# The head of a two-block transformer kernel: its set-up stages become the beginning of the input projection's stage

## What is computed

```python
def rmsnorm(x, g, eps=NORM_EPS):
    xf = x.astype(jnp.float32)
    y = xf * lax.rsqrt(jnp.mean(xf * xf, axis=-1, keepdims=True) + eps)
    return (y * g.astype(jnp.float32)).astype(x.dtype)

def modulate(h, shift, scale):
    return h * (1.0 + scale) + shift

def adaln(cond, w_mod, b_mod):
    return jax.nn.silu(cond) @ w_mod + b_mod
...
        mod = adaln(c, w_mod[l], b_mod[l])[:, None, :]
        mod_c = adaln(c_ctx[None, :], w_mod[l], b_mod[l])[:, None, :]
...
        h = modulate(rmsnorm(x, p['g_pre_mix']), sh1, sc1)
        h_c = modulate(rmsnorm(ctx, p['g_pre_mix']), sh1c, sc1c)
        y, y_c = token_mixer(h, h_c, p, lam_init, cos, sin, need_ctx)
```

## Time and profile before

| | us |
|---|---|
| median of 3 runs | 3788.89 |
| the runs | 3785.69 to 3792.41 |
| the profiled execution's own time | 3778.42 |
| its span from the first instruction to the last | 3776.4 |

### The profile page before, as it was taken

The page is one execution under the profiler, slowest core; times in us unless marked ns, Lnnn a source line. Parts: engine busy times, 40 slices in busy tenths (PEclk is TensorE's granted clock), DMA queues, the critical chain, the costliest instruction groups (busy, mean ns, idle before and its releaser), DMA issues.

```text
span 3776.4 us, 71939 instructions
## 1 busy us (share of the span) xinstructions
PE 3500.4 (93%) x30972; PEld 3214.3 (85%) x30972; DVE 2033.0 (54%) x3196; ACT 1569.3 (42%) x2561; POOL 122.8 (3%) x233
## 2 busy tenths in 40 slices
PE   5299987999988998999999999999999999999997
PEld 2288776988987877887888999989999999999997
DVE  1447775878774774553434687332224653344665
ACT  0455664444433773443333555211114443333553
POOL 0000000000000000100000011000000100000011
PEclk8599998999998998999999999999999999999998
DMA  4223344232323403321111565211113421111664
GB/s 149 83 79 127 119 149 171 88 105 88 104 74 67 93 1 113 122 79 51 45 51 56 188 210 189 77 28 45 45 45 108 134 84 46 45 45 56 196 218 140
DMA packets 323386, 369.44 MB, mean 98 GB/s; under 512 B 14189, under 2 KB 262716, under 8 KB 323070
## 3 DMA queue, kind: packets, MB, share of 16 engines
q1 hardware_dynamic: 306958, 311.48, 26.8%
q0 software_dynamic: 16112, 53.37, 4.2%
HBM read 303.84 MB, written 60.95 MB: 97 GB/s over the span
## 4 chain that ended last, share of the span: by engine, by line
PE 55%; DVE 3%; ACT 2%; issue 1%; DVEq 0%; DMA 0%; POOL 0%; ACTq 0%
PE psum L3252 10%; PE psum L3253 9%; PE psum L3254 9%; PE psum L2331 4%; PE psum L2806 4%; PE psum L2332 4%; PE psum L2333 4%; PE psum L2807 4%; PE psum L2808 4%; PE psum L2668 1%; DVE u_val L3452 1%; DVE w_lo L3153 1%; PE psum L3199 1%; ACT u_val L3343 0%; DVE g L3457 0%
## 5 line engine op out<-in xcount | busy, mean ns | idle before, releaser
L3252 PE MATMUL psum<-mix_h_hi,w_hi 128*128 128x342 f32 (+5 forms) x1848 | 636.1, 344 | 17.1 <-DVE w_lo L3153 15.2
L3253 PE MATMUL psum<-mix_h_hi,w_lo 128*128 128x342 f32 (+5 forms) x1848 | 632.1, 342 | 0.0
L3254 PE MATMUL psum<-mix_h_lo,w_hi 128*128 128x342 f32 (+5 forms) x1848 | 631.6, 342 | 0.0
L2198 DVE TENSOR_TENSOR w_lo<-w_raw,w_hi 128x1024 fp32r<-128x1024 f32 (+1 forms) x167 | 195.8, 1172 | 398.0 <-ACT w_hi L2188 396.5
L3252 PEld LDWEIGHTS psum<-mix_h_hi,w_hi 128*128 128x128 f32 x1848 | 348.9, 189 | 47.4 <-DVE w_lo L3153 18.6
L2188 ACT ACTIVATE w_hi<-w_raw 128x1024 fp32r<-128x1024 f32 (+1 forms) x167 | 170.3, 1020 | 487.7 <-PE psum L2808 325.3
L3254 PEld LDWEIGHTS psum<-mix_h_lo,w_hi 128*128 128x128 f32 x1848 | 348.8, 189 | 26.9
L3253 PEld LDWEIGHTS psum<-mix_h_hi,w_lo 128*128 128x128 f32 x1848 | 349.0, 189 | 26.2
L737 PE MATMUL psum<-h_hi,w_hi 128*128 128x512 f32 (+1 forms) x592 | 228.3, 386 | 49.2 <-DVE w_lo L899 49.2
L2331 PE MATMUL psum<-down_ghi,w_hi 128*128 128x256 f32 x944 | 269.8, 286 | 0.4 <-DVE down_glo L2203 0.2
L3329 ACT ACTIVATE xs<-psum 128x1024 f32<-128x1024 f32 (+1 forms) x66 | 67.8, 1028 | 486.4 <-PE psum L3254 486.4
(11 more groups left out here) (437 smaller groups left out, 8064.6 us busy)
## 6 DMA issues: line engine op xcount, KB each, us to landing
w_raw<-in_w_down SPq DMA_DIRECT2D x118, 512.0 KB, 3.9
w_raw<-in_w_up SPq DMA_DIRECT2D x110, 512.0 KB, 3.8
w_raw<-in_w_in SPq DMA_DIRECT2D x59, 512.0 KB, 4.0
down_w_raw<-in_w_down SPq DMA_DIRECT2D x58, 512.0 KB, 3.9
unit<-rw_operands SPq DMA_DIRECT2D x40, 512.0 KB, 6.8
rw_operands<-step_set SPq DMA_DIRECT2D x16, 1024.0 KB, 6.4
mod_w<-in_w_mod POOLq DMA_DIRECT2D x32, 512.0 KB, 5.8
w_raw<-in_w_out SPq DMA_DIRECT2D x32, 512.0 KB, 4.0
```

Source lines behind the costliest of these rows:

```text
L3252: nc.tensor.matmul(out, k.w_hi[:, s, w], xh[:, kk, x], start=(kk == 0), stop=False)
L3253: nc.tensor.matmul(out, k.w_lo[:, s, w], xh[:, kk, x], start=False, stop=False)
L3254: last = nc.tensor.matmul(out, k.w_hi[:, s, w], xl[:, kk, x], start=False, stop=(kk == KD - 1))
```

## The change

The six stages are gone. Their work is written into the class `Front`, whose methods are called at the head of each engine's list in `in_projection`, so that no barrier stands between them and the first tile:

- SP asks for token rows first: five 512 KB buffers (RING), then the four parameter vectors that are needed early (72 rows, EARLY), the other five tiles, three groups of `w_mod` (three buffers), the first `w_raw`, the fourth group, and then the store of x and the constants. The other 36 parameter vectors are asked for by POOL.
- PE turns the ten tiles of tokens first, then spreads the factors, then sums the modulation rows.
- ACT no longer copies halves of `xT` (DVE copies whole tiles). It squares the token rows as they land, with a sum along the row (`accum_out`), so the channel tiles are neither squared nor added up, and PE's sums over channels (L362) are gone.
- DVE multiplies x by the spread factors straight from PSUM into `x_hat`, for all eight tiles and before the modulation is known. `rbc` is not written.
- Scale and shift are applied in place on `x_hat`, even tiles by DVE and odd ones by ACT. Tile 0 of the projection takes the channel tiles as the outer loop and its three pieces inside, and waits for each `h_lo` (`lowered`).
- The late parameter rows are turned between the modulation sums and tile 0, and copied to `prm` by DVE after the last `h_lo`. DVE's `weight_low(1)` and its preparations stand behind that.
- The two memsets of `xs` are gone. Tiles 1 to 25 and all later stages are as they were.

The diff, cut to its core:

```diff
+    def sync(self, sp, first_weights):
+        k = self.k
+        for n in range(self.RING):
+            self.load_tile(sp, n)
+        sp.wait_ge(self.ident_set, 1)
+        for name, src, n, at in self.early:
+            sp.dma_start(self.stage[at:at + n, 0, :], src).then_inc(self.early_landed, 16)
+        for n in range(self.RING, self.n):
+            self.load_tile(sp, n)
+        for n in range(3):
+            self.load_mod(sp, n)
+        first_weights(0)
+        self.load_mod(sp, 3)
+        sp.wait_ge(self.kept, self.n)
+        sp.dma_start(*tiles_of(k.x_dram, k.xT[:, :, CTX:ALL])).then_inc(self.x_stored, 16)
...
+    def scalar_early(self, act):
+        nc, k = self.nc, self.k
+        for n in range(self.n):
+            act.wait_ge(self.row_landed[n % self.RING], 16 * (n // self.RING) + 16)
...
+            nc.scalar.activation(self.junk[n % 2][:, :], self.rows[n % self.RING][:, :], ACT.Square,
+                                 accum_out=k.stat[:, 0, n:n + 1]).then_inc(self.squared, 1)
...
+    def scalar_late(self, act):
+        nc, k = self.nc, self.k
+        act.wait_ge(self.mod_kept, 5)
+        for kk in range(KD):
+            if kk % 2:
+                for c0, c1, gain, shift in self.sides(kk):
+                    nc.scalar.activation(self.hat(kk, c0, c1), self.hat(kk, c0, c1), ACT.Identity, bias=shift, scale=gain)
+                act.drain()
+            else:
+                act.wait_ge(self.shifted, kk // 2 + 1)
+            nc.scalar.activation(k.h_hi[:, kk, :], self.hat(kk, 0, ALL), ACT.Copy).then_inc(self.high, 1)
...
+    def vector_late(self, dve):
+        nc, k = self.nc, self.k
+        self.shift(dve, 0)
+        for kk in range(KD):
+            if kk % 2 == 0 and kk + 2 < KD:
+                self.shift(dve, kk + 2)
+            self.lower(dve, kk)
+        dve.wait_ge(self.late_turned, 1)
...
+        dve.drain().then_inc(self.late_kept, 1)
+        dve.wait_ge(self.x_stored, 16)
...
-            for n in range(TOTAL):
+            front.tensor(pe)
+            pe.wait_ge(w_low, 1)
+            for kk in range(KD):
+                pe.wait_ge(front.lowered, kk + 1)
+                w = slice(kk * P, (kk + 1) * P)
+                for j, (c0, cn) in enumerate(pieces(0)):
...
+            pe.wait_ge(front.late_kept, 1)
+            pe.wait_ge(front.tables, 32)
+            for n in range(1, TOTAL):
...
-            weight_low(0)
-            weight_low(1)
...
-    setup_stage(nc, k)
-    adaln_stage(nc, k, "mod1", 0, 16)
-    load_turned(nc, k, "x", [(ins["ctx"][0], CTX, 0), (ins["x"][0], SEQ, CTX)], k.xT)
```

More of the change, by code:

```diff
@@ L148, in rows_of @@
     return k.prm[:, c:c + 1] if isinstance(c, int) else k.prm[:, bass.ds(c, 1)]
[L151 to L204, removed]
@@ L220, in adaln_turn @@
     return last
[L223 to L274, removed]
@@ L277, in load_turned @@
[L277 to L296, removed]
-                pe.wait_ge(landed[n % 2], 16 * (n // 2 + 1))
-                if n >= 2:
-                    for half in kept:
-                        pe.wait_ge(half, n - 1)
-                for kk in range(KD):
-                    last = nc.tensor.transpose(k.psum[:, 2 * (n % 2) + kk // 4, (kk % 4) * P:(kk % 4) * P + m],
-                                               rows[n % 2][0:m, kk * P:(kk + 1) * P], k.ident[0:m, 0:m])
-                last.then_inc(turned, 1)
-        def halves(half):
-            for n, (src, m, at, r) in enumerate(tiles):
-                out = dst[:, 4 * half:4 * half + 4, at + r:at + r + m]
-                src_ps = k.psum[:, 2 * (n % 2) + half, :].rearrange("p (a b) -> p a b", a=4)[:, :, 0:m]
-                yield n, out, src_ps
-        @block.vector
-        def _(dve):
-            for n, out, src_ps in halves(0):
-                dve.wait_ge(turned, n + 1)
-                nc.vector.tensor_copy(out, src_ps).then_inc(kept[0], 1)
-        @block.scalar
-        def _(act):
-            for n, out, src_ps in halves(1):
-                act.wait_ge(turned, n + 1)
-                nc.scalar.activation(out, src_ps, ACT.Copy).then_inc(kept[1], 1)
@@ L592, in stores @@
                     store_centred(p, s - 1)
-            weights(0)
+            front.sync(sp, weights)
             sp.dma_start(k.cos[:, :], k.ins["cos_k"]).then_inc(tables, 16)
@@ L723, in after_piece @@
                         mean(p, s - 2)
-            for n in range(TOTAL):
+            front.tensor(pe)
+            pe.wait_ge(w_low, 1)
+            for kk in range(KD):
+                pe.wait_ge(front.lowered, kk + 1)
+                w = slice(kk * P, (kk + 1) * P)
+                for j, (c0, cn) in enumerate(pieces(0)):
+                    x, out = slice(c0, c0 + cn), k.psum[:, j, 0:cn]
+                    mm(out, k.w_hi[:, 0, w], k.h_hi[:, kk, x], start=(kk == 0), stop=False)
+                    mm(out, k.w_lo[:, 0, w], k.h_hi[:, kk, x], start=False, stop=False)
+                    last = mm(out, k.w_hi[:, 0, w], k.h_lo[:, kk, x], start=False, stop=(kk == KD - 1))
+            last.then_inc(acc_done, 1)
+            pe.wait_ge(front.late_kept, 1)
+            pe.wait_ge(front.tables, 32)
+            for n in range(1, TOTAL):
                 s = n % 2
@@ L1030, in rope_low @@
                     in1=k.qk_hi[:, 0:m].bitcast(F32), op0=ALU.mult, op1=ALU.subtract).then_inc(worked, 1)
+            front.vector_early(dve)
+            weight_low(0)
+            front.vector_late(dve)
+            weight_low(1)
             c = k.col["k_a"]
@@ L1101, in first_block @@
     k.xT = k.at("x_t", [KD, ALL], k.BIG)
[L1103 to L1106 removed]
+    k.h_hi = k.at("h1_hi", [KD, ALL], 104576, F32R)
     k.h_lo = k.at("h1_lo", [KD, ALL], 104576 + KD * ALL * 4, F32R)
     assert k.top <= k.limit, (k.top, k.limit)
[L1109 to L1119 removed]
     in_projection(nc, k)
```

291 lines of the change are left out of this document (177 added, 114 removed).

## The result

| | us |
|---|---|
| the changed kernel, median of 4 runs | 3677.48 (3673.22 to 3683.83) |
| the kernel before beside it, median of 4 runs | 3790.65 (3785.69 to 3794.36) |
| ratio | 0.9704, 95% interval 0.9684 to 0.9723 |
| the changed kernel's profiled execution, its span | 3679.61, 3677.6 |
| the profiled execution before, its span | 3778.42, 3776.4 |

The kernel is 113 us faster by these medians and 99 by the two profiled executions. The forecast was 97, and its range ended at 3681, 3.5 us too high. Two things have to be found: where the head differs from the forecast, and why two ways of comparing differ by 14 us.

The account below looks back on a forecast made before the run. PE bounds the kernel from tile 1 on, after a head of one-engine stages. Tile 1 moves from 186.3 to 88.4 (24.1 + 3.4 + 3.9 + 32.05 + 25), less 1.0 debt: 3788.9 - 96.9 = 3692, range 3681 to 3707.

Parts of the forecast that it names:

- The turning: Head's start: PE transposes ten token tiles at the low clock, 1.70 us each, from 5.3 us; last copy at 24.1.
- the scatter of the runs: Whole-time range: the runs' own scatter was allowed 3 us at each end.
- The bound and the question: Whole kernel: PE bounds it from tile 1 on, so an earlier tile 1 (186.3 to 88.4) moves everything behind it forward.
- T: Time in the head when the last copy of xT ends, forecast at 24.1 us.
- The rival: Turning in the head: the clock rises among transposes, copies set the pace, T 3 us earlier, total 3689; chance 0.14.
- From T to the modulation: Head: PE idle 3.4 us, spreading matmuls 3.9, modulation sums 32.05; modulation complete at 63.4, no w_mod load in the path.
- From the modulation to tile 1: Head's end: ACT's rounding, scale and shift chain (18.0), then w_lo of tile 1; 25 us, so tile 1 at 88.4.
- The debt: Behind tile 1's start: tile 2's weights come late through single-buffered w_raw, delaying sigmoid and gate product; loss 1 us (0 to 4).
- The low-clock rival for tile 0: Tile 0 of the projection: PE runs it at the low clock, eight channel tiles take 25.6 us, total 3698; chance 0.12.
- POOL's transfers: Late parameter rows: 36 issues at 0.51 us, landed in time; rival of late rows, at 6 us each 3840, chance 0.02.
- the rule of the Trainium skill that the prediction weighed: POOL's 36 transfers: VectorE in a 2-port mode locks GpSimd out of its SBUF rings, which speaks against moving them there.
- The sum and the range: Whole time: 97.9 less 1.0 gives 96.9 us off the median 3788.9, so 3692; range 3681 to 3707.

## Why the prediction was off, point by point

Two terms of the sum failed. The turning was priced with every transpose at the low clock, 1.70 us a tile, and this made it 3.5 us too long. And the scatter of the runs was put at 3 us, where executions of one kernel lie 26 us apart. The points in order:

- **The bound and the question.** Right: the gain is the shift of tile 1, and apart from scatter everything behind it moved as one block. The forecast of that shift was 97.9, measured 103.0. The spans from tile 1 to the end were to be equal within 2 us, and in the two profiles they differ by 4.2 (3590.1 and 3594.2); this too is scatter, of a size that the prediction didn't allow for.
- **The turning (T = 24.1, measured 19.9).** Two terms. The first tile landed 0.7 us sooner than taken. The larger, 3.5 us, was the pace: 1.70 us a tile at the low clock, where the turning took 14.1 us of PE's time from its first transpose to its last, and not 17.6. This is the step that was wrong in its mechanism. The rival had it, with T = 21.2 and a chance of 0.14, and it happened. The rows read for it, 80 transposes at 0.50, showed transposes with gaps of 0.7 to 2.0 us behind the first 16, and I had noted that the change takes the gaps away. The runs with two and five buffers, in either kernel, show that this decides. The rival was off in part in what sets the pace once the clock is up, the copies by its account. They do stand close together, DVE being busy 9.3 of the 10 us from 8 to 18, but from 11.95 on PE waited four times for token rows (1.3 us in all), and the last tile's turning began at 17.56, as its row landed. The working had that landing at 17.7. So with the clock up the transfers, at some 400 GB/s by the windows, set the end of the turning.
- **From T to the modulation (39.35, measured 39.7).** Right in its path, and its sum is right since two errors cancel: PE waited 2.8 us from T to the spreading where 3.4 was taken, the spreading took 4.63 where 3.9 was taken, all of it at 0.50, and the modulation sums 32.3 instead of 32.05. No transfer of w_mod was late; the products x_hat were done at 38.7, before the second group's additions.
- **From the modulation to tile 1 (25, measured 23.7).** The mechanism was right, ACT's chain and then the meeting of PE's end and `w_lo` of tile 1, 0.35 us apart. ACT's pair of scale and shift took 1.72 (rows 6 gave 1.83 as a sum of two durations, and they overlap by a little at their ends), four times, and the whole of ACT's chain 16.9 where 18.0 was taken. The small sums of this part run 0.1 to 0.2 over their terms; nothing hangs on that.
- **The debt (1 us, measured as PE's wait of 0.6).** Right in kind. The low-clock rival for tile 0 did not happen: the clock was back at 1.00 before its third channel tile.
- **POOL's transfers.** Issued at 0.51 to 0.54 each beside a busy DVE (the first took 0.66, the last 0.58), and PE didn't wait for the late rows. The row of one parameter's three transfers:

```profile
L256 POOL DMA_DIRECT2D param_rows<-in_conv_w_ffn x3 | 1.5, 516 | 0.0
```

  DVE's work there was mostly copies out of PSUM. Which of its instructions run in a 2-port mode no view here shows, so the rule of the Trainium skill that the prediction weighed stays untested.
- **The sum and the range.** This step failed outright. I wrote 3 us for the runs' own scatter, from three runs 7 us apart, and took the 10.5 us between profile and median as if it were a constant. Executions of this kernel lie 26 us apart, and a median of four can be 5 off. The measured median lies 14.5 us below the forecast: 5.1 by the head's term, 0.4 by the debt, 5.4 because the first comparison's four runs lay that far below their kernel's pooled mean, 1.4 because the 3788.9 started from lies above the pooled mean of the kernel before, and some 2 that the pooled means leave open. The head alone, or the draw alone, would have stayed in the range. The range was also added up 1 us wide at both ends: its terms give 3682 and 3706. That the profiled execution came within 2 us of the 3681.5 forecast for it is luck, as the head won 5 us more and the stages behind it lost 4.

What the parts are worth, each undone alone in the changed kernel, by the start of tile 1: squares on the token rows 18.9, own stage 20.8 (of which the loop order of tile 0 is 14.0), five buffers 13.1. They make 53 of the 103. The other 50 were not undone one by one: neither the order of turning and modulation sums nor the products with the factors ahead of the modulation has a run of its own. By the traces, and this is a reading and not shown by a run, they are the 28.64 us before the first modulation product, which now hold the turning; the modulation itself, which took from 122.5 to 161.3 in small pieces handed to and fro and now takes 59.6 to 81.0; and the barriers.

## What to carry to other kernels

Where a program begins with stages in which one engine at a time works, write their waits in one line and sum what stays between the first transfer and the first product that the bound engine needs; here the rest of the program followed one to one, but for scatter. When a change removes the gaps of the matrix engine, take its pace at both clock levels, since rows from a stretch with gaps don't say which it will be, and then ask anew what bounds the stretch: here it was the landing of the rows. And before a range is drawn, look at how far executions of the same kernel lie apart, and judge small steps by a landmark in the trace that repeats.

## What the runs showed of the hardware

- With the token rows in five buffers, 128x128 fp32 transposes without gaps raised the granted clock from 0.50 to 1.00 in the middle of a program, behind 4.71 us of idleness (durations of 273 instead of 421 ns). At the start of a program the durations fell in the same way. 28 more transposes kept it up to the next matmuls (2.42 us at 1.00), where without them it fell to 0.50 in 4.08 us of idleness (4.63 us). With waits of 0.7 to 2.0 us ahead of each tile from the third on the clock stayed at 0.50 for ten tiles (the kernel before), and with 0.4 to 2.0 the durations stayed at 421 ns (two buffers in the changed kernel).
- At the start of these programs the record of the granted clock isn't to be relied on: it stood at 1.00 up to 33 us while 80 transposes took 421 ns each.
- Executions of the kernel before differed by up to 26 us of 3787, and the difference went with the mean granted clock (0.953 to 0.962, correlation -0.92 and -0.96). In the profiles of both kernels it lay in all parts behind the head: 580.5 to 590.7 us for the recurrent stage, 412.2 to 416.8 for the projection from its tile 1 on, 2590.6 to 2596.2 for all behind.
